# PEER expert layers: from three dense token tiles and two by rows to two dense and three by rows

## What is computed

```
q = h @ w_q                      # per token 8 heads x 2 halves of 128
s = q . keys                     # 128 scores for each of the 16 (head, half) codes
sv, si = top16(s)                # per code
best, bi = top16(sv0 + sv1)      # per head, over the 256 sums
expert = i1 * 128 + i2           # 8 x 16 = 128 experts per token, out of 16384
gate = softmax(best)
act = gelu(h . u[expert]) * gate
out = sum over the 128 experts of act * v[expert]
```

## Time and profile before

| | us |
|---|---|
| median of 3 runs (5298.86 to 5309.67) | 5304.23 |
| the profiled execution, its own time | 5300.41 |
| its span, first to last instruction | 5298.6 |
| PE busy / DVE / POOL / ACT | 4684.5 / 3207.6 / 1870.7 / 768.3 |
| loop over chunks, layer 0 / layer 1 | 1264.6 / 1268.5 |
| bytes moved by DMA | 1048.91 MB |

### The profile page before, as it was taken

How to read it: one execution, slowest core, us unless ns; L and a number is a source line. 1 busy time by engine, 2 the same in 40 slices (tenths; PEclk the granted TensorE clock), 3 DMA queues, 4 the chain that set the end, 5 groups by cost and what they waited for, 6 DMA issues and landing times. The chain is left out here.

```text
span 5298.6 us, 46397 instructions
## 1 busy us (share of the span) xinstructions
PE 4684.5 (88%) x15368; PEld 2582.2 (49%) x15368; DVE 3207.6 (61%) x6158; ACT 768.3 (15%) x1541; POOL 1870.7 (35%) x1753
## 2 busy tenths in 40 slices
PE   7796778868879999999998898869879999999997
PEld 2452222236565554555543577627564554555543
DVE  4435888817972675666577422537972675666477
ACT  1200111101181000000000222211180000000000
POOL 0001665400181364655454000000190464555464
PEclk8898888889999999999999898879999999999998
DMA  3110222132164798999997120021264898999897
GB/s 129 48 74 34 80 79 79 60 48 92 60 171 134 288 362 314 402 351 364 342 356 302 60 66 22 7 82 61 66 182 135 301 369 318 387 358 357 316 386 276
DMA packets 362456, 1048.91 MB, mean 198 GB/s; under 512 B 39977, under 2 KB 140601, under 8 KB 350554
## 3 DMA queue, kind: packets, MB, share of 16 engines
q0 software_dynamic: 148128, 545.35, 27.2%
q1 hardware_dynamic: 115068, 450.86, 23.7%
q10 hardware_dynamic: 99072, 50.33, 3.4%
HBM read 992.29 MB, written 54.14 MB: 197 GB/s over the span
## 5 line engine op out<-in xcount | busy, mean ns | idle before, releaser
L598 PE MATMUL banks<-blocks,dense_weight 128*128 128x512 f32 x3072 | 1376.3, 599 | 51.9 <-DVE dense_weight L773 51.8
L565 PE MATMUL banks<-h_dense_T,blocks 128*128 128x384 f32 x4096 | 1363.5, 487 | 37.7 <-DVEq L666 37.7
L565 PEld LDWEIGHTS banks<-h_dense_T,blocks 128*128 128x128 f32 x4096 | 779.8, 191 | 628.7 <-issue 111.1
L598 PEld LDWEIGHTS banks<-blocks,dense_weight 128*128 128x128 f32 x3072 | 589.0, 192 | 755.2 <-issue 696.9
L409 POOL DMA_INDIRECT expert_rows<-in_pk_u_dram,expert x512 | 649.7, 1269 | 796.8 <-DVE own_dots L788 351.9
L409 POOL DMA_INDIRECT expert_rows<-in_pk_v_dram,expert x512 | 598.9, 1170 | 493.7 <-DVE acc L807 207.8
L773 DVE TENSOR_TENSOR dense_weight<-dense_act,shared 128x384 f32<-128x384 f32 x256 | 218.6, 854 | 806.1 <-PE banks L598 741.7
L807 DVE SCALAR_TENSOR_TENSOR acc<-expert_rows,expert_weight,acc 128x1024 f32<-128x1024 f32 x504 | 623.8, 1285 | 61.4 <-DMA expert_rows<-in_pk_v_dram,expert 60.9
L788 DVE CUSTOM_DVE_ANT_0 expert_rows<-expert_rows,h_rows 128x1024 f32<-128x1024 f32 x512 | 595.1, 1221 | 0.1
L444 ACT ACTIVATE dense_act<-banks 128x384 f32<-128x384 f32 x256 | 125.7, 491 | 2356.4 <-PE banks L565 2356.4
L400 POOL TENSOR_SCALAR shared<-iota,picked_T 128x128 f32<-128x128 f32 x192 | 120.9, 645 | 521.2 <-ACT picked_T L450 459.3
(11 more groups left out here) (423 smaller groups left out, 5288.4 us busy)
## 6 DMA issues: line engine op xcount, KB each, us to landing
blocks<-in_pk_u_turned_dram SPq DMA_DIRECT2D x256, 512.0 KB, 6.3
blocks<-in_pk_v_dram SPq DMA_DIRECT2D x256, 512.0 KB, 6.7
gates_dram<-shared ACTq DMA_DIRECT2D x48, 1024.0 KB, 5.1
shared<-gates_dram SPq DMA_DIRECT2D x32, 1536.0 KB, 10.5
ada_block<-in_ada_rest_dram SPq DMA_DIRECT2D x32, 1280.0 KB
blocks<-in_pk_w_q_dram SPq DMA_DIRECT2D x32, 512.0 KB, 3.9
w_block<-in_ev_w_in_dram SPq DMA_DIRECT2D x16, 512.0 KB, 3.3
expert_rows<-in_pk_u_dram,expert POOLq DMA_INDIRECT x512, 7.7
```

The lines of the kernel that those rows point to most:

```text
L565: mm = pe.matmul(dense_dots(c), u[:, k * P:(k + 1) * P], HT[:, k, :], start=(k == 0), stop=(k == KD - 1))
L598: mm = pe.matmul(ps[:, at_:at_ + HALF], wt[:, c % WEIGHED, z * P:(z + 1) * P], v[:, half_ * HALF:(half_ + 1) * HALF], start=(c == 0), stop ...
```

## The change

Tile 2 moves from the dense tiles to the row tiles: two dense tiles (256 tokens), three by rows. The pacing starts with chunk 0 and gives 6 1/8 rows a chunk. One of the three row searches (that of the first row tile, now tile 0 with index ND = 2) is taken out of the loop and put between the second one-hots of the two dense tiles on DVE, with its exponential on ACT between the two spreads. `shared` grows by 1024 columns a partition, since the transposed row tiles need three; the gate buffers and query buffers follow the new widths.

```
-DENSE_TILES = (2, 3, 4)
-ROW_TILES = (0, 1)
+DENSE_TILES = (3, 4)
+ROW_TILES = (0, 1, 2)
-FIRST_ROWS = 16
@@ rows_by
-    n = max(0, c + 1 - FIRST_ROWS)
-    return min(2 * SLOTS * NR, 4 * n + 2 * n // 3)
+    return min(2 * SLOTS * NR, 6 * (c + 1) + (c + 1) // 8)
@@ buffers
-        shared = buf(ctx, nc, "shared", [P, 3 * 2 * D])
+        shared = buf(ctx, nc, "shared", [P, 7 * D])
-        HTR = shared[:, 2 * D:4 * D].rearrange("p (k t) -> p k t", k=KD)
+        HTR = shared[:, 2 * D:5 * D].rearrange("p (k t) -> p k t", k=KD)
         first_hot = [h.rearrange("p (b n) -> p b n", n=P)
-                     for h in (shared[:, 4 * D:5 * D], acc[:, 0, :])]
+                     for h in (shared[:, 5 * D:6 * D], acc[:, 0, :])]
         second_hot = [h.rearrange("p (b n) -> p b n", n=P)
-                      for h in (shared[:, 5 * D:6 * D], acc[:, 1, :])]
+                      for h in (shared[:, 6 * D:7 * D], acc[:, 1, :])]
-        gate_in = [shared[:, b * 3 * D:(b + 1) * 3 * D] for b in range(2)]
+        gate_in = [shared[:, b * ND * D:(b + 1) * ND * D] for b in range(2)]
-        qc = [dense_act[:, 2 * c:2 * c + 2, :] ...
+        qc = [dense_act[:, 3 * c:3 * c + 3, :] ...
@@ ScalarE
-            for z in range(ND):
-                spread_tile(z)
+            spread_tile(0)
+            exponentials(ND)
+            spread_tile(1)
@@ VectorE
-            for z in range(ND):
-                second_hots(z)
-            last = (x for i in range(ND, NT) for x in by_head(i))
+            second_hots(0)
+            for _ in by_head(ND):
+                pass
+            second_hots(1)
+            last = (x for i in range(ND + 1, NT) for x in by_head(i))
```

More of the change, by code:

```diff
@@ L323, in experts @@
         gain, scale, shift, junk = rows[:, 0, :], rows[:, 1:3, :], rows[:, 3:5, :], rows[:, 5, :]
-        qc = [dense_act[:, 2 * c:2 * c + 2, :].rearrange("p b n -> p (b n)") for c in range(2)]
+        qc = [dense_act[:, 3 * c:3 * c + 3, :].rearrange("p b n -> p (b n)") for c in range(2)]
         at_f = rest[:, 0, :].rearrange("p (a s) -> p a s", a=2)
```

## The result

After: **5387.49 us** median of 4 runs (5378.49 to 5390.07), before 5302.18 (5298.86 to 5309.67, 4 runs); ratio 1.0154, 95% interval 1.0138 to 1.0170. The change makes the kernel 1.5% slower. 5349 was forecast, 45 us over the kernel before, and 85 came. The sign and the bound of the loop hold, and the cost is nearly twice what was forecast.

What follows compares the result with a forecast made beforehand. DMA bytes were to bound the new loop: 1309 + 5 + 13 + 23 = 1350 us against 1266.6, less 61 saved elsewhere, +22.4 a layer, +45 for two, so 5349 us; 8 in 10 range 5278 to 5450.

Steps and rivals of the forecast that it cites:

- rival A: Byte bound alone: GpSimd's gathers always in time in the loop, 1327 us a layer, kernel 5303 us; chance 20%.
- search and early dots: Ahead of the loop: sums for two dense tiles and dots with 256 columns let the spread begin 30.2 us earlier.
- spread with moved search: Ahead of the loop: two dense tiles' spreads with one row search between them take 119.8 us instead of 139.9.
- the search's price: In the spread: PE and POOL wait some 32 us a layer for the moved search, which the old loop hid.
- dots 12 to 15 and first gates: Last stretch before the loop: four chunks at 3.45 us and smaller gate loads, 19.9 us instead of 28.2.
- loop, bytes: Loop after the first weigh: 535.9 MB of gathers, blocks and gates at 410 GB/s, 1309 us a layer.
- loop, start: Loop start: ring rows are freed only after chunk 0's weigh and three search steps, 5 us a layer.
- loop, gathers and side steps: In the loop: 3% of the rows' pace in half of them plus heavy search steps, 23 us a layer.
- loop, end: Loop end: last row's work, three adds, weigh and the sums of chunks 126 and 127, 13 us a layer.
- B: Second tile's one-hots take 37 us instead of 44 and the loop's start loses nothing: kernel 5280 us; chance 15%.
- C: GpSimd bounds the loop's u rows, every gather meeting a row operation: 96 us a layer more, kernel 5495; chance 17%.
- D: TensorE loses its clock in the loop: every chunk at 1.2 GHz, +356 us a layer, kernel 6016; chance 3%.

Runs made afterwards that it cites:

- the new split alone: The changed kernel with all three row searches back in the loop, four side steps a chunk, rows from chunk 16 at 7 a chunk: 5435.94 us.
- the run without side steps: The changed kernel without the two searches in the loop, row tiles 1 and 2 reusing row numbers and weights of tile 0: 5359.48 us.
- light dots: The changed kernel with DVE's dot of each u row over 128 of its 1024 columns, all bytes still fetched: 5364.91 us.
- half the bytes: The changed kernel with each gather fetching only the first half of its row, same number of gathers and row operations: 5055.71 us.
- the doubled dots: The changed kernel with TensorE computing the dots of chunks from 16 on twice, into the same bank: 5389.13 us.

## Why the prediction was right, and where it was short

*The question asked was the right one.* The sum itself has a slip: 535.9 MB at 410 GB/s are 1307 us and not 1309, which would have made the forecast 5345. The 410 GB/s from short full stretches of the old trace turned out to be the rate of some 1100 of the new loop's 1354 us (403 to 410), and u rows reach it as well as v rows, which rival A's "against" doubted. Bytes forecast 535.9, moved 537.2 MB. Term by term, in us a layer:

| step | forecast | measured |
|---|---|---|
| search and early dots | -30.2 | -29.3 / -31.3 (start of stage to spread: 270.0 / 272.3 before, 240.7 / 241.0 after) |
| spread with moved search | 139.9 to 119.8 | 122.9 |
| of it the search's price | 32 | 29.7 |
| dots 12 to 15 and first gates | 28.2 to 19.9 | **28.7** |
| loop, bytes | 1309 | 1310 |
| loop, start | 5 | 7.9 |
| loop, gathers and side steps | 23 | 18.5 |
| loop, end | 13 | 17.0 |
| whole | +22.4 | +41.2 / +36.6 |

*The failed step* is "Four chunks at 3.45 and two gate loads of 1 MB ... 19.9". It counted PE's work and the gate load, and left out what the change starts beside them: with row numbers known ahead of the loop, GpSimd gathers ten rows, 5 MB, in just this stretch. The run with the gathers put behind the gates shows the cause, and the new split alone, which has no early rows, shows the forecast to be right for itself: there the stretch takes 19.9 us. The prediction's bounds of 52 to 68 us a layer, which count the adds behind the loop, didn't hold 48.0 and 49.9; without these adds it is 45.6 and 47.5. "Less than 50" from the stages ahead was one of its two signs of being wrong, and that sign came; the other, a loop under 1325 or over 1380, did not. Of the 19 and 14 us a layer that the forecast was short, 8.8 are this, 3.1 the spread and 4 to 5 the loop; the rest is how the layers of before differ from their mean (1264.6 and 1268.8 in the loop, 270.0 and 272.3 ahead of the spread).

*Start and end.* At the start DVE has weigh, a 2.3 us step and ten waiting rows while GpSimd waits for its first free buffer, for 24 us in all; I counted only the steps after the first weigh. At the end the last row lands some 17 us ahead of the last sum.

*GpSimd's 23 us.* Nearly the right size for partly the wrong reason, so that it came near 18.5 is in part luck. A steady 3% loss of pace in the u rows isn't there: between 2000 and 2800 some 3 us are lost, and the u gathers of the loop wait 87.1 us for own_dots, the sign that the prediction gave to rival A. The loss lies in the two dips, where the heavy steps stand beside rows, as both the run without side steps (-11 and -14) and that with light dots (-7) show; the 23 had them as "a little".

*Rivals.* A (20%) had the right bound without these losses; the kernel is outside it. B (faster) needed 409 GB/s over the whole loop and 66 us saved outside it, and had 397 and 48 to 50. C is refuted by half the bytes: 1200 us with the same gathers. D: the granted clock did fall, in the loop from 0.99 to 0.88, and cost nothing, as the doubled dots show. The likeliest reason, only argued, is the one given: an engine that waits has room for it. The dots at 380 ns were as forecast; the sums' 743 ns in place of 599 come with the waits and the lower clock (which of the two isn't parted), and lie in PE's slack: it is busy 981 of 1354 us, where 870 was forecast.

*Left open.* How much of the spread's 3 us is GpSimd's start. What a wait of the gathers for both the write and the first load of the gates would bring wasn't tried.

## What to carry to other kernels

Before work is moved from an engine to a transfer, divide the loop's bytes by the best rate that short full stretches of the old trace show, and add what goes missing at the two ends; here that gave 1310 of 1354 us. When something is ready earlier, ask what it will run beside: ten early gathers delayed a small write on which the first step hung. And look at both sides of a balance first: here five rows a chunk and a gelu three chunks earlier won 1% where the new split lost 1.5%.

## What the runs showed of the hardware

- One core's DMA moved 404 GB/s in the mean over 1310 us on end (1610 to 2920 of after), gathers and block loads mixed, and 409 or 410 in the stretches where nothing held the gathers up. That is the ceiling of this mix in these loops (up to 416 in single 20 us windows) and not of the DMA: the loads at the start of after moved 425 in 15:35.
- Beside a burst of ten gathers (q0 in the page: 813.82 MB in 221856 packets, some 3.7 KB each) a 1 MB write in packets of 508 B (q10: 33.56 MB in 66048) ended 22.9 us after its issue, in place of a median of 5.1. With the gathers behind it, it ended after 4.9.
- A gather's issue takes GpSimd 0.94 us alone, up to 1.99 beside DVE's row operations, and 2.02 to 2.85 beside a two-input step of 2.3 us: most that meet such an operation end 0.81 us after it. Beside a reduction as long it takes 0.94. With DVE dots of 0.29 us the mean falls from 1315 to 985 ns.
- TensorE's granted clock in the loop (1.00 is the full 2.4 GHz) went 0.99, 0.88, 0.96 with PE busy 1246 of 1265, 981 of 1354 and 1268 of 1359 us; from the second of these loops to the third, both bound by bytes, the clock rose and the time stayed within 5.3 us.
